# Slots of two experts packed feature-major in one product per tile, and a first up projection that starts on half of the features

## The chip, the cores and the metric

The kernel runs on one core of a Trainium2 chip. The time is that of the device, in microseconds (us), and the profile is one execution of the program. TensorE multiplies matrices, VectorE and ScalarE do elementwise work and evict TensorE's results from its accumulator banks, GpSimd (POOL) and SyncE mostly issue transfers, and 16 DMA engines carry these out. Everything is float32. The profile names TensorE's products PE and its weight loads PEld; the stationary operand of a product is what is loaded, the moving operand streams past it.

## The reference

The reference is one inference step of a two-layer encoder on 288 tokens (256 of a prompt, 32 of a sample) of width 1024. Each layer has an attention part and then a mixture of experts: 16 experts in 4 groups, of which each token uses two.

```
for e in range(N_EXPERTS):
    h = jax.nn.silu(t @ w_gate[e]) * (t @ w_up[e])
    y = y + gate[:, e:e + 1] * (h @ w_down[e])
```

The expert weights (6 MB per expert, 96 MB per layer) are by far the largest input. `gate` is zero except for the two chosen experts of a token, so an expert's product need only be made for the tokens routed to it.

## The kernel before

Tokens lie in three tiles (`TOKS`): 128, 128 and 32 rows of `x_tok`, a token per partition, 1024 features along it. After the attention part, TensorE computes router logits (`route`), and VectorE picks the two experts of each token. For each expert up to 64 tokens are gathered into slots (`CAP = 64`).

The slots of an expert must be there with features on partitions (`xg`, 128 features of 8 blocks by 64 slots), since the features are what the up projection sums over. For experts 2 to 15 the tokens are sorted through DRAM: POOL waits for `sort_row` (L1799), scatters the rows with six indirect DMAs (L2035), loads them back sorted (L2038, L2039, 2.36 MB), TensorE turns them (`turn_rows`, L951), and ScalarE cuts each expert's slots out.

For experts 0 and 1 that would come too late. Their slots are made by products with a 0/1 matrix `pick` (token by 128 slots, 64 of each expert), which VectorE writes last thing before the path in question (L1788). `pack_first` (L935) makes it in two steps. First, for each half of the features, three products (one per token tile) with `pick` stationary and 512 features moving give the slots with tokens on partitions (L939). ScalarE and VectorE copy a half each to `x_first` (L1415, L1801). TensorE runs one filler product of 512 columns (L942, shown at its helper's line L686), transposes the 8 blocks of `x_first` (L948), and ScalarE and VectorE copy the results into `xg` (L1417, L1803). Only then expert 0's up projection starts (`up`, L963, and `expert_up`, L912): 8 feature blocks by 2 halves of the array's columns, products of 512 columns, L916.

The order of the experts' work is written out (`expert_order`): up 0, up 1, down 0, turn the sorted rows, down 1, up 2, then up e and down e - 1 in turn.

Expert weights go into three buffers each for gate and up (4 MB per expert) and for down (2 MB). SyncE issues the loads in the same order (L553 to L559): those of experts 0 to 2 early, that of expert e + 3 when expert e's up projection (`up_done`) or down projection is through. So the load of expert 3's gate and up waits for the end of expert 0's up projection.

## Time and profile before

| | |
|---|---|
| runs, us | 913.27, 915.42, 921.26 (median 915.42) |
| profiled execution, span | 916.5 us, 9955 instructions (the page gives no time of its own around it) |
| TensorE busy | 793.1 us (87%) |
| VectorE, ScalarE, POOL busy | 335.0, 187.3, 44.0 us |
| DMA | 272.80 MB, mean 298 GB/s |
| chain that ended last | PE 56%, DMA 25%, DVE 9%, SyncE's queue 6% |
| mean granted TensorE clock | 0.953 |

Busy time is counted per engine, whether or not something waited for it. The chain that ended last is followed back from the last instruction to what released each step; it says on whom the time depended. The granted clock is the share of TensorE's 2.4 GHz that it was given; its two levels are 1.00 and 0.50 (1.2 GHz).

### The profile page before, as it was taken

Reading aid. Unit: us, or ns where it says so; the run is one execution under the profiler, and the core shown is the slowest. Engines: PE = TensorE matmul, PEld = TensorE weight load, DVE = VectorE, ACT = ScalarE, POOL = GpSimd, SP = SyncE. Lnnn points to the kernel's source line nnn. Section 1 sums busy time; section 2 is a strip of 40 time slices with the busy share of each in tenths; the row PEclk is TensorE's granted clock in tenths of the full one; section 3 lists DMA queues with packets and bytes.
Section 4 is the critical chain, followed back from the end, with each engine's and each line's share of the span. In section 5 each row is a group of like instructions: output and inputs, shape, how many; then the busy total and the mean of one; then the engine's idle time right before and its main releaser. Section 6 shows DMA issues by size and latency. Waiting matters only on the chain.

```text
span 916.5 us, 9955 instructions
## 1 busy us (share of the span) xinstructions
PE 793.1 (87%) x3943; PEld 387.2 (42%) x3943; DVE 335.0 (37%) x749; ACT 187.3 (20%) x452; POOL 44.0 (5%) x58
## 2 busy tenths in 40 slices
PE   6978999998899886876879989979898999777875
PEld 4665777453433222222334567654534333222221
DVE  1016455445422212122281054654533442122138
ACT  1213343110321101110110025620103211111101
POOL 1012000003000000000100000000020000000020
PEclk9998899899999999998989999999989999999998
DMA  9724007736999999999799060581679999999991
GB/s 357 232 72 196 1 1 297 300 153 239 402 424 423 425 428 422 425 426 424 265 350 361 3 261 1 215 330 53 275 282 424 431 423 429 422 428 423 428 398 57
DMA packets 43552, 272.80 MB, mean 298 GB/s; under 512 B 6360, under 2 KB 11166, under 8 KB 25840
## 3 DMA queue, kind: packets, MB, share of 16 engines
q1 hardware_dynamic: 32032, 243.69, 64.6%
q0 software_dynamic: 5888, 19.95, 6.5%
q10 hardware_dynamic: 5584, 8.51, 2.6%
q8 instruction: 32, 0.52, 0.2%
q14 instruction: 16, 0.13, 0.0%
HBM read 253.92 MB, written 18.21 MB: 297 GB/s over the span
## 4 chain that ended last, share of the span: by engine, by line
PE 56%; DMA 25%; DVE 9%; SPq 6%; ACT 2%; issue 1%; ACTq 0%; DVEq 0%
DMA arena<-in_expert_w_up 24%; PE bank L916 16%; PE bank L858 6%; PE bank L930 5%; PE bank L1176 5%; PE bank L845 3%; SPq L502 2%; PE bank L832 2%; PE bank L777 2%; PE bank L939 2%; PE bank L1049 2%; PE bank L825 1%; PE bank L679 1%; PE bank L1141 1%; PE bank L868 1%
## 5 line engine op out<-in xcount | busy, mean ns | idle before, releaser
L916 PE MATMUL bank<-arena 128*64 128x512 f32 x1024 | 240.7, 627 | 48.2 <-DMA arena<-in_expert_w_up 46.5
L916 PEld LDWEIGHTS bank<-arena 128*64 128x64 f32 x1024 | 77.2, 144 | 208.4 <-issue 148.8
L930 PE MATMUL bank<-arena 128*64 128x512 f32 x512 | 116.9, 598 | 16.7 <-DVE arena L1825 16.7
L1825 DVE COPY arena<-bank 128x256 f32<-128x256 f32 x32 | 13.6, 424 | 271.8 <-PE bank L923 271.8
L930 PEld LDWEIGHTS bank<-arena 128*64 128x64 f32 x512 | 34.1, 136 | 77.4 <-issue 54.6
L1378 ACT ACTIVATE arena<-bank 128x256 f32<-128x256 f32 x32 | 12.3, 384 | 265.8 <-PE bank L916 265.8
L1833 DVE RECIPROCAL arena<-arena 128x256 f32<-128x256 f32 x32 | 56.1, 1753 | 1.1
L858 PE MATMUL bank<-arena 128*128 128x512 f32 x128 | 56.0, 595 | 0.0
L1176 PE MATMUL bank<-arena 128*128 128x512 f32 x96 | 43.9, 619 | 6.6 <-ACT arena L1483 5.7
L1234 ACT COPY arena<-bank 128x512 f32<-128x512 f32 (+2 forms) x30 | 15.8, 537 | 112.9 <-PE bank L679 74.2
L858 PEld LDWEIGHTS bank<-arena 128*128 128x128 f32 x128 | 24.0, 190 | 29.6 <-issue 29.5
L1400 ACT COPY arena<-bank 128x512 f32<-128x512 f32 x30 | 17.6, 587 | 91.6 <-PE bank L930 91.6
L845 PE MATMUL bank<-arena 128*128 128x288 f32 x128 | 33.2, 412 | 0.0
L1382 ACT COPY arena<-arena 128x512 f32 x28 | 31.4, 1128 | 8.0 <-issue 7.2
L1176 PEld LDWEIGHTS bank<-arena 128*128 128x128 f32 x96 | 18.9, 199 | 30.3 <-issue 23.4
L1523 DVE COPY arena<-bank 128x512 f32<-128x512 f32 (+3 forms) x20 | 12.9, 649 | 49.5 <-PE bank L679 17.9
L679 PE MATMUL bank<-arena 128*128 128x128 f32 (+1 forms) x144 | 23.1, 320 | 8.0 <-DVE arena L1988 3.2
L1049 PE MATMUL bank<-arena 128*128 128x512 f32 x64 | 28.0, 595 | 1.0 <-DVE arena L1523 1.0
L2024 POOL DMA_DIRECT2D arena<-in_ln_g x4 | 2.3, 567 | 534.6 <-ACT arena L1382 313.5
L845 PEld LDWEIGHTS bank<-arena 128*128 128x128 f32 x128 | 23.7, 190 | 8.5 <-issue 2.7
L679 PEld LDWEIGHTS bank<-arena 128*128 128x128 f32 (+1 forms) x144 | 20.9, 202 | 13.8 <-issue 4.3
L777 PE MATMUL bank<-arena 128*128 128x64 f32 (+1 forms) x172 | 24.0, 280 | 1.3 <-DVE arena L1682 0.5
(272 smaller groups left out, 870.1 us busy)
## 6 DMA issues: line engine op xcount, KB each, us to landing
arena<-in_expert_w_gate SPq DMA_DIRECT2D x32, 2048.0 KB, 20.6
arena<-in_expert_w_up SPq DMA_DIRECT2D x32, 2048.0 KB, 25.6
arena<-in_expert_w_down SPq DMA_DIRECT2D x64, 1024.0 KB, 27.9
arena<-in_w_out SPq DMA_DIRECT2D x4, 2048.0 KB, 9.5
expert_rows<-arena ACTq DMA_DIRECT2D x60, 128.0 KB, 7.9
arena<-in_w_kv_shared SPq DMA_DIRECT2D x3, 2048.0 KB, 10.5
arena<-in_w_mem_kv SPq DMA_DIRECT2D x2, 2048.0 KB, 21.1
arena<-sorted_rows POOLq DMA_DIRECT2D x2, 2048.0 KB, 9.2
```

The lines of the kernel that those rows point to most:

```text
L502: sp.dma_start(g_kv, ins["kv_norm_g"][0].partition_broadcast(P)).then_inc(small_in, 16)
L679: last = tr(b[:, k * n:(k + 1) * n], src[0:n, t, k0 + k::KC], ident[0:n, 0:n])
L777: last = mm(b[:, qt * w:(qt + 1) * w], pt[:, P * i:P * i + P], v[:, kt, h * w:(h + 1) * w], start=(i, kt) == mine_[0], stop=(i, kt) == min ...
L832: last = mm(b[:, 0:NT], w_q[:, k, 4 * g + hh, :], cq_feat[:, k, :], start=k == 0, stop=k == 2)
L845: last = mm(b[:, 0:NT], w_inb[k // 4][:, k % 4, P * c:P * c + P], x_feat[:, k, :], start=k == 0, stop=k == KC - 1)
L858: last = mm(b[:, :], x_feat[:, k, P * t:P * t + P], w_out[k // 4][:, k % 4, 512 * c:512 * (c + 1)], start=k == 0, stop=k == KC - 1)
L916: last = mm(bank[j][64 * half:64 * half + 64, :].rearrange("p (u f) -> p u f", u=2), slots[:, k, 0:CAP], w[:, :, k, 256 * half:256 * half ...
L930: last = mm(bank[3 + j][64 * n:64 * n + 64, :], hid_t[:, j, c, 64 * half:64 * half + 64], w[:, half, c, 512 * n:512 * n + 512], start=(hal ...
L1049: last = mm(b[:, :], feat[:, k, P * t:P * t + P], w[:, k, :], start=k == 0, stop=k == KC - 1)
L1176: last = mm(b[:, :], x_feat[:, k, P * t:P * (t + 1)], w_kvs[c][:, k, :], start=k == 0, stop=k == KC - 1)
L1382: return nc.scalar.copy(xg[:, j], xs[:, bass.ds(at, CAP), :].rearrange("p s k -> p k s"))
L1833: step(V.reciprocal(a, a))
```

## The change

`pack_first` makes the slots feature-major at once: for each of the 8 feature blocks and each token tile, 128 features of `x_tok` (every eighth one) are stationary and the 128 columns of `pick` move. The three products of a block add up in a quarter of an accumulator bank; four blocks fill bank 7, four bank 5. The step over `x_first`, its two copies, the filler product and the transposes go. The first up projection takes its first four feature blocks after ScalarE's copy and waits for VectorE's only before the other four. The second (`up(1)`) has no wait of its own, since it comes behind the first on the same engine.

```
-            def expert_up(j, w, slots):
+            def expert_up(j, w, slots, ks=range(KC)):
-                for k in range(KC):
+                for k in ks:
...
             def pack_first(l):
                 for half in range(2):
-                    for t, (a, n) in enumerate(TOKS):
-                        last = mm(bank[5 + half][:, :], pick[0:n, t, :], x_tok[0:n, t, 512 * half:512 * half + 512],
-                                  start=t == 0, stop=t == 2)
-                    last.then_inc(packed, 1)
-                keep_warm(bank[1], 512)
-                for n, who in enumerate("av"):
-                    pe.wait_ge(first_taken[who], 2 * l + 1)
-                for half in range(2):
                     b = bank[(7, 5)[half]]
                     for k in range(4):
-                        last = tr(b[:, P * k:P * k + P], x_first[:, 4 * half + k::KC], ident)
-                    last.then_inc(first_turned, 1)
+                        for t, (a, n) in enumerate(TOKS):
+                            last = mm(b[:, P * k:P * k + P], x_tok[0:n, t, 4 * half + k::KC], pick[0:n, t, :],
+                                      start=t == 0, stop=t == 2)
+                    last.then_inc(first_packed, 1)
...
-                    if e < 2:
-                        for who in "av":
-                            pe.wait_ge(first_taken[who], 2 * (l + 1))
-                    else:
+                    if e == 0:
+                        for half, who in enumerate("av"):
+                            pe.wait_ge(first_taken[who], l + 1)
+                            last = expert_up(0, ups[0], xg[:, 0], range(4 * half, 4 * half + 4))
+                        last.then_inc(up_done, 1)
+                        return
+                    if e > 1:
                         pe.wait_ge(xg_ready, (NE - 2) * l + e - 1)
...
-                ac.wait_ge(packed, 2 * l + 1)
-                nc.scalar.copy(x_first[:, 0:512], bank[5][:, :]).then_inc(first_taken["a"], 1)
-                ac.wait_ge(first_turned, 2 * l + 1)
+                ac.wait_ge(first_packed, 2 * l + 1)
                 nc.scalar.copy(*first_dst(0)).then_inc(first_taken["a"], 1)
...
-                ve.wait_ge(packed, 2 * l + 2)
-                V.tensor_copy(x_first[:, 512:D], bank[6][:, :]).then_inc(first_taken["v"], 1)
-                ve.wait_ge(first_turned, 2 * l + 2)
+                ve.wait_ge(first_packed, 2 * l + 2)
                 V.tensor_copy(*first_dst(1)).then_inc(first_taken["v"], 1)
```

## Rows read from the trace of the kernel before

**Rows 1.** The page, its first line.
```profile
span 916.5 us, 9955 instructions
```

**Rows 2.** The chain of waits in time: start us, length us, what.
```profile
302.49 32.94 DMA arena<-in_expert_w_up
...
836.78 41.35 DMA arena<-in_expert_w_up
```

**Rows 3.** Windows: stretch, length, busy us per engine, granted clock, DMA share, GB/s.
```profile
227.50:231.50 4.00, 4.00 (x21) 1.56 (x18) 0.61 (x4) 0.09 (x1) 0.07 (x1) 1.00 0.84 291
235.00:236.50 1.50, 1.50 (x10) 0.69 (x8) 0.00 (x0) 0.00 (x0) 0.00 (x0) 1.00 0.76 210
236.50:300.00 63.50, 59.65 (x291) 23.04 (x289) 20.75 (x30) 16.25 (x21) 0.52 (x1) 1.00 1.01 426
300.00:431.00 131.00, 100.75 (x430) 32.24 (x428) 30.78 (x48) 17.78 (x26) 1.09 (x2) 0.95 1.01 425
...
674.50:681.00 6.50, 6.34 (x30) 2.65 (x32) 3.31 (x19) 0.00 (x0) 0.00 (x0) 1.00 0.98 341
681.00:684.50 3.50, 3.50 (x18) 1.38 (x16) 2.23 (x3) 0.38 (x1) 0.00 (x0) 1.00 0.75 174
```

**Rows 4.** Timeline of layer 0's path: start us, length us, engine, line, what.
```profile
214.40 7.00 PE L939 MATMUL bank<-arena 128*128 128x512 f32 x12 [0.45 <-DVE arena L1788]
...
223.45 0.69 DVE L1803 COPY arena<-bank 128x512 f32<-128x512 f32 x1 [1.31 <-PE bank L948]
224.06 0.94 DVE L1805 TENSOR_SCALAR starts<-arena 1x16 int32<-1x16 f32 x5
224.29 13.95 PE L916 MATMUL bank<-arena 128*64 128x512 f32 x64 [0.88 <-DVE arena L1803]
...
231.41 0.33 SPq L528 DMA_DIRECT2D arena<-in_expert_w_gate  x1
```

**Rows 5.** Timeline of layer 1's path.
```profile
661.41 10.37 PE L939 MATMUL bank<-arena 128*128 128x512 f32 x12 [0.58 <-DVE arena L1788]
...
674.66 13.95 PE L916 MATMUL bank<-arena 128*64 128x512 f32 x64 [0.88 <-DVE arena L1803]
...
681.78 0.33 SPq L528 DMA_DIRECT2D arena<-in_expert_w_gate  x1
```

**Rows 6.** Timeline of TensorE's weight loads, both packs, then the routing counts.
```profile
218.91 0.19 PEld L939 LDWEIGHTS bank<-arena 128*128 128x128 f32 x1 [0.24 <-issue]
219.34 0.19 PEld L939 LDWEIGHTS bank<-arena 128*128 128x128 f32 x1 [0.24 <-issue]
220.28 0.29 PEld L939 LDWEIGHTS bank<-arena 32*128 32x128 f32 x2 [0.76 <-issue]
221.34 0.30 PEld L686 LDWEIGHTS bank<-arena 128*128 128x128 f32 x2 [0.76 <-issue]
...
662.43 0.33 PEld L939 LDWEIGHTS bank<-arena 128*128 128x128 f32 x1 [0.52 <-issue]
663.28 0.33 PEld L939 LDWEIGHTS bank<-arena 128*128 128x128 f32 x1 [0.52 <-issue]
665.12 0.50 PEld L939 LDWEIGHTS bank<-arena 32*128 32x128 f32 x2 [1.50 <-issue]
667.12 0.50 PEld L939 LDWEIGHTS bank<-arena 128*128 128x128 f32 x2 [1.50 <-issue]
...
211.57 0.84 PEld L908 LDWEIGHTS bank<-arena 128*128 128x128 f32 x6
```

**Rows 7.** Windows of stretches at half clock, columns as in rows 3.
```profile
213.10:216.40 3.30, 2.85 (x5) 0.96 (x4) 2.53 (x13) 0.00 (x0) 0.00 (x0) 0.50 0.06 25
660.20:670.40 10.20, 9.62 (x11) 2.84 (x10) 2.45 (x13) 0.59 (x1) 5.26 (x6) 0.50 0.48 191
663.60:667.00 3.40, 3.40 (x4) 0.51 (x3) 0.00 (x0) 0.00 (x0) 2.77 (x3) 0.50 0.49 194
158.50:165.20 6.70, 6.15 (x48) 4.50 (x50) 1.51 (x4) 2.83 (x4) 0.00 (x0) 0.50 1.00 411
431.50:434.90 3.40, 3.40 (x10) 0.95 (x8) 0.00 (x0) 0.00 (x0) 0.00 (x0) 0.50 1.02 425
```

More of the change, by code:

```diff
@@ L264, in encoder_step @@
         y_out = zr.cut(2, 512)
-        x_first = Region(y_at).cut(D)
         pair_t = zr.cut(NT)
@@ L309, in encoder_step @@
         tail_ready = sem("tail_ready")
-        packed = sem("packed"); first_turned = sem("first_turned")
+        first_packed = sem("first_packed")
         first_taken = {"a": sem("first_taken_act"), "v": sem("first_taken_dve")}
```

## The prediction

> **What bounds the kernel now.** I read the chain of waits first. In each mixture-of-experts stage it is TensorE until about 302 us (layer 0) and 752 us (layer 1), and from there it is made of waits for expert weights, such as the two in [rows 2]. The windows say why: from 236.5 to 300 us the DMA engines move 426 GB/s and from 300 to 431 us 425 GB/s, without a hole [rows 3]. The loads cannot be shortened, only started earlier. The first load of the saturated stream (expert 3's gate and up weights) is issued by SyncE when expert 0's up projection ends, at 231.41 us and at 681.78 us [rows 4, 5]. So the change is worth what it does to the end of that projection, less what the DMA engines would have been doing anyway.
>
> They were doing something: POOL's load of the sorted rows (576 rows of 4 KB, 2.36 MB). In layer 1 it starts at 674.5 us; 341 GB/s over 6.5 us is 2.22 MB, so it ends near 681.35. The weights come 0.4 us after that, and the 3.5 us from 681 run at 174 GB/s instead of 426 [rows 3]: 3.5 x (1 - 174/426) = 2.07 us lost. In layer 0 it has 1.16 MB by 231.5 (291 GB/s over 4 us) and alone would end near 234.4, three microseconds after the weights are issued; there only 1.5 x (1 - 210/426) = 0.76 us is lost [rows 3]. Call these two losses the slack: no gain can be larger than their sum, 2.8 us.
>
> **The path that changes.** Before: packing starts at 214.40 (layer 0) and 661.41 (layer 1), and expert 0's first product at 224.29 and 674.66: 9.89 and 13.25 us [rows 4, 5]. Packing itself is 7.0 and 10.4 us; the remaining 2.95 us are the filler product, eight transposes and two evictions, the last of which is the 0.69 us of [rows 4]. All of these 2.95 us go.
>
> What comes: 24 products of 128 columns instead of 6 of 512, each again two weight loads and two passes. The columns streamed are the same; the loads are four times as many, 48 instead of 12, and, above all, the order over the token tiles is 128, 128, 32 rows for each of eight feature blocks, where before it was run through twice. [Rows 6] price that. At full clock a pass of 512 columns takes 219.34 - 218.91 = 0.43 us, thus 0.107 us for 128 columns. The two passes on the tile of 32 rows take 221.34 - 220.28 = 1.06 us from load to load, where 0.86 would be the columns: leaving a row size costs 0.20 us. At half clock: 663.28 - 662.43 = 0.85 a pass (0.213 for 128 columns), and 667.12 - 665.12 = 2.00 for two, thus 0.29 per change. That the cost does not shrink with the product is shown by six passes of only 16 columns over the same three tiles (last row of that group): their loads alone take 0.84 us.
>
> A block of features is then 6 passes and 2 changes of row size: 6 x 0.107 + 2 x 0.20 = 1.04 us at full clock, 6 x 0.213 + 2 x 0.29 = 1.86 us at half. Eight blocks: 8.3 us or 14.9 us. The bounds: changes cost nothing (5.1 and 10.2 us), or each change also exposes one more load of 0.107 or 0.213 us (10.0 and 18.3 us). I take the middle, since it is what the rows with both product sizes give.
>
> **Which clock?** The clock decides. It was at half from before the pack in both layers, for 3.4 us in layer 0 and for 10.2 us in layer 1 [rows 7]. In layer 0 it came back after TensorE had run products on all 128 rows up to 216.4. In layer 1 it stayed at half through a stretch in which TensorE had no idle time, but in which half of the passes were on 32 rows (663.6 to 667.0), and came back after the next one, on 128 rows. It also stayed at half through transposes that end on the 32-row tile (158.5 to 165.2) and came back at once after dense expert products (431.5 to 434.9) [rows 7]. The new pack is, without a stop, what it stayed low in: every third product is on 32 rows, and there are two gaps in each block. So I forecast half clock for the whole pack, and for the first 3.4 us of expert 0's up projection, as in 431.5 to 434.9. The other outcome is the first rival.
>
> The Trainium skill ("TensorE: Matmul & The Clock Gate", Part 1) says that the default state is throttled and sustained activity releases it. By that rule, dense work releases it within the pack and the sum is that of rival 1; layer 1's 10.2 us of nearly unbroken work at half clock [rows 7] speak against leaning on it here.
>
> **The sum.** Pack 14.9 us and 0.1 us to the first product: 15.0 against 9.89 and 13.25, thus +5.1 and +1.75 us. The projection itself takes 13.95/2 = 6.97 us at full clock [rows 4]; 3.4 us at half add 1.7. It ends 6.8 and 3.45 us later, and the loads are issued at 238.2 and 685.2 us. Through the DMA: in layer 1 the issue was 0.4 us behind the end of the row load and 2.07 us were lost, so loss = lateness + 1.65. Layer 0: 238.2 - 234.4 + 1.65 = 5.45, less the 0.76 of before: +4.7. Layer 1: 685.2 - 681.35 + 1.65 = 5.5, less 2.07: +3.4. Together +8.1 us, 916.5 -> 924.6 us on the scale of the profiled span [rows 1]. The median of the runs, 915.42, lies 1.1 us below it, so 923.5 us.
>
> Costed at nothing, with their covers. Splitting expert 0's projection: ScalarE's eviction of the first four blocks (0.6 us) hides behind the second half of the pack, VectorE's (0.69 us) behind the projection's first half, at least 3.5 us; uncovered, 0.7 us more. What VectorE does behind that eviction (start columns and flag, some 4 us after 224.06) moves to about 230 to 234.5; its next reader is past expert 0's activation at 238. The sort and the row load hang on VectorE and POOL alone and don't move. Later, TensorE is 4 to 7 us late at turning the rows and at down 0 and 1, but the 8.4 MB of experts 3 and 4 take 20 us, and the next issues come inside them. The late TensorE then waits less at 302 and 752 us.
>
> **Rivals.**
> 1. *The clock comes back inside the pack, as now.* Layer 0: half clock until 216.4, 1.1 blocks, then 6.9 x 1.04: the first product at 223.8, 0.5 us early. Layer 1: half until 670.4, 4.85 blocks, then 3.3 us: 673.8, 0.9 us early. At most 1.4 us gained: 914.0 us. For it: it did so in both layers, and where the filler before the pack falls well it needs little more. Against: the 663.6 to 667.0 stretch. If it happens in one layer only, 4 to 5 us of my sum go: 918 to 919 us. Chance 0.26, most of it for one layer.
> 2. *Changes of row size cost nothing in short products.* Layer 0: 24 products at 0.213 us each and the half-clock part give 220.6; layer 1 gives 671.2; both about 3.5 us early, and denser, so that the clock behaves as now. The gain is capped by the slack: 2.8 us, 912.6 us. Against it stands the last row of [rows 6]. The Trainium skill says both things: its TensorE page (Part 2, Step-by-step) lets the next weights load during the running product, with a time set by columns and not rows, which gives this rival; "TensorEngine Tiling (Array Packing)", Key Properties, says that a change of tiling mode drains the engine, and that is what [rows 6] show. Chance 0.07.
> 3. *Half clock through the whole projection too.* 15.0 + 13.9 us: issues at 243.3 and 690.3 us, 9.8 and 8.5 us lost: 933.7 us. The clock returned sooner in every dense expert stretch of the trace. Chance 0.07.
>
> On the other side of my forecast stands rival 1, in both layers. It decides at the point where the clock is back before the fourth block: 6.9 to 7.0 us of pack is then reachable again.
>
> **How the numbers follow.** Forecast 0.60, 923.5 us; its own range is 919 to 927 us (a pack of 13.5 to 16 us, 2.5 to 6 us of half clock in the projection, in each layer). The range reported is 914 to 927 us: it takes in rival 1 and leaves out rivals 2 and 3 and the tails. A change of over 1%, which is about what a measurement of this kernel can tell from none (its runs spread from 913.27 to 921.26), means below 906.3 or above 924.6 us. Below: no case reaches it, as the slack is 2.8 us; 0.02. Above: rival 3 and somewhat over a quarter of the forecast, 0.23. Within: 0.75.
>
> **What would show it.** In the profile after: 24 products per layer at the new packing line over 14 to 16 us (8 to 9 says rival 1, 5 to 6 says rival 2), weight loads with 0.2 or 0.3 us extra at each tile of 32 rows; a granted clock of 0.50 through the pack and 3 to 4 us on; expert 3's load issued at about 238 and 685 us; a hole in the DMA windows of both layers, about 4 us longer than now in layer 0. The forecast is wrong if the clock is at full speed during the pack, or if the stream of weights starts as early as now.

## The result and the profile after

The changed kernel took 934.89 us (median of 4 runs, 931.67 to 940.89) against 914.35 us (4 runs, 912.94 to 921.26). The medians are 20.5 us apart, a quotient of 1.0225; the ratio on record, which is not that quotient, is 1.0186 with a 95% interval of 1.0129 to 1.0244. Two further measurements of the same kernel, below, gave ratios of 1.0181 and 1.0151, with medians 14.8 and 13.7 us apart. So it is slower by 1.5 to 1.9%, some 14 to 20 us, and outside the predicted range of 914 to 927 us. The direction, and the first product and the load issue both coming later, were as forecast; the size was not.

The profiled execution is the longest of its four runs. These lines of its page are the first one (answering to [rows 1]), the row of engines, the granted clock in 40 slices and the chain by engine:

```profile
span 939.1 us, 10051 instructions
...
PE 822.9 (88%) x3995; PEld 411.5 (44%) x3995; DVE 333.1 (35%) x747; ACT 186.2 (20%) x450; POOL 44.1 (5%) x58
...
PEclk9997899986899989888889999989869999999988
...
PE 58%; DMA 24%; DVE 8%; SPq 6%; ACT 2%; issue 1%; ACTq 0%; DVEq 0%
```

Of the 22.6 us between the two profiled spans, not all is the change. The pack starts at 220.52 us here, 6.1 us later than in [rows 4], behind code that is the same in both kernels: TensorE was at half clock from 203 to 216 us (first row of the windows below). Other executions of the changed kernel start it at 211.8 and 211.3 us, so these 6.1 us belong to this execution and not to the kernel.

The timelines of the two paths, which answer to [rows 4, 5]:

```profile
220.52 16.02 PE L940 MATMUL bank<-arena 128*128 128x128 f32 x48 [0.83 <-DVE arena L1782]
...
236.47 15.66 PE L915 MATMUL bank<-arena 128*64 128x512 f32 x64
...
245.31 0.33 SPq L527 DMA_DIRECT2D arena<-in_expert_w_gate  x1
...
678.41 16.24 PE L940 MATMUL bank<-arena 128*128 128x128 f32 x48 [0.23 <-DVE arena L1782]
...
694.59 15.29 PE L915 MATMUL bank<-arena 128*64 128x512 f32 x64
...
703.06 0.33 SPq L527 DMA_DIRECT2D arena<-in_expert_w_gate  x1
```

From the start of the pack to the first product of the projection it is 15.95 and 16.18 us (9.89 and 13.25 before), and to the issue of expert 3's load 24.8 and 24.65 us (17.0 and 20.4 before). Windows (stretch, length, busy time of TensorE, its loads, VectorE, ScalarE, POOL, then granted clock, DMA share, GB/s) ahead of the first pack, over both packs and over the stretch behind each, which answer to [rows 3, 7]:

```profile
203.00:216.00 13.00, 12.50 (x33) 8.16 (x34) 5.80 (x22) 0.84 (x3) 0.00 (x0) 0.50 0.97 411
216.00:222.90 6.90, 6.07 (x30) 4.41 (x29) 4.08 (x22) 0.00 (x0) 0.12 (x1) 0.99 0.02 8
222.90:239.90 17.00, 17.00 (x49) 11.45 (x50) 2.91 (x14) 0.59 (x1) 6.91 (x8) 0.50 0.71 263
240.00:246.00 6.00, 6.00 (x32) 1.96 (x30) 1.28 (x6) 0.39 (x1) 0.00 (x0) 1.00 0.20 39
676.90:697.30 20.40, 20.16 (x58) 13.47 (x58) 5.01 (x25) 0.59 (x1) 7.03 (x8) 0.50 0.59 217
697.40:704.00 6.60, 6.60 (x34) 2.11 (x32) 2.11 (x10) 0.38 (x1) 0.00 (x0) 1.00 0.17 48
```

In layer 1 the clock is at its half level (0.50) through the whole pack and on into the projection; in layer 0 of this execution the first 2.4 us of the pack, up to 222.9, are at full clock and the rest at half. The pack is hardly shorter for it: 15.96 us to the first product, against 16.17 where all of it is at half. Behind it, the DMA engines carry 39 and 48 GB/s while the sorted rows are in and expert 3's weights are not yet asked for. The weight loads inside the pack, in layer 1 (answering to [rows 6]):

```profile
678.41 1.03 PEld L940 LDWEIGHTS bank<-arena 128*128 128x128 f32 x4 [1.66 <-DVE arena L1782]
...
679.67 0.55 PEld L940 LDWEIGHTS bank<-arena 32*128 32x128 f32 x2 [0.22 <-issue]
680.44 1.03 PEld L940 LDWEIGHTS bank<-arena 128*128 128x128 f32 x4 [0.22 <-issue]
681.70 0.55 PEld L940 LDWEIGHTS bank<-arena 32*128 32x128 f32 x2 [0.22 <-issue]
682.46 1.04 PEld L940 LDWEIGHTS bank<-arena 128*128 128x128 f32 x4 [0.22 <-issue]
```

A block of features takes 680.44 - 678.41 = 2.03 us; the forecast was 1.86.

**Where the time went.** I cut every profiled execution at the same points: start of the pack (P), first product of expert 0 (U), issue of expert 3's load (I), start of expert 15's up projection (the last long wait for weights ends there), start of the next layer's pack, end. All in us:

| kernel | span | layer: U - P | I - P | P to last up | last up of layer 0 to pack of layer 1 | last up of layer 1 to end |
|---|---|---|---|---|---|---|
| before | 916.5 | 9.9 / 13.3 | 17.0 / 20.4 | 216.3 / 216.8 | 230.7 | 38.4 |
| after | 939.1 | 16.0 / 16.2 | 24.8 / 24.6 | 222.0 / 221.8 | 235.9 | 38.9 |

The difference of the spans is 6.1 (ahead of the pack) + 5.7 + 5.2 + 5.0 + 0.5 = 22.5 us. The two layers' 10.7 us were forecast as 8.1. The 5.2 us between the last up projection of layer 0 and the pack of layer 1, where no instruction was changed, were forecast as nothing.

### The profile page after: what moved, and what is told of

Read it like the earlier page. It is cut to its first block, busy times and chain, and to the rows that moved or that the text cites. A ratio compares the mean times of both kernels' runs of the same rounds, so it can differ in the third digit from the quotient of the medians.

```text
span 939.1 us, 10051 instructions
## 1 busy us (share of the span) xinstructions
PE 822.9 (88%) x3995; PEld 411.5 (44%) x3995; DVE 333.1 (35%) x747; ACT 186.2 (20%) x450; POOL 44.1 (5%) x58
## 4 chain that ended last, share of the span: by engine, by line
PE 58%; DMA 24%; DVE 8%; SPq 6%; ACT 2%; issue 1%; ACTq 0%; DVEq 0%
DMA arena<-in_expert_w_up 23%; PE bank L915 16%; PE bank L857 6%; PE bank L929 5%; PE bank L1172 5%; PE bank L940 3%; PE bank L844 3%; SPq L501 2%; PE bank L831 2%; PE bank L776 2%; PE bank L1045 2%; PE bank L678 1%; PE bank L824 1%; PE bank L1137 1%; PE bank L685 1%
## 5 line engine op out<-in xcount | busy, mean ns | idle before, releaser
L915 PE MATMUL bank<-arena 128*64 128x512 f32 x1024 | 246.5, 639 | 44.2 <-DMA arena<-in_expert_w_up 44.2
L929 PE MATMUL bank<-arena 128*64 128x512 f32 x512 | 116.9, 598 | 16.6 <-DVE arena L1817 16.6
L1817 DVE COPY arena<-bank 128x256 f32<-128x256 f32 x32 | 13.6, 424 | 272.1 <-PE bank L922 272.1
L857 PE MATMUL bank<-arena 128*128 128x512 f32 x128 | 56.0, 595 | 0.0
L1172 PE MATMUL bank<-arena 128*128 128x512 f32 x96 | 44.6, 626 | 6.6 <-ACT arena L1477 5.7
L857 PEld LDWEIGHTS bank<-arena 128*128 128x128 f32 x128 | 24.0, 190 | 29.6 <-issue 29.5
L940 PE MATMUL bank<-arena 128*128 128x128 f32 (+1 forms) x96 | 32.3, 492 | 1.1 <-DVE arena L1782 1.1
L1172 PEld LDWEIGHTS bank<-arena 128*128 128x128 f32 x96 | 19.1, 201 | 30.7 <-issue 23.8
L678 PE MATMUL bank<-arena 128*128 128x128 f32 (+1 forms) x144 | 24.4, 332 | 7.9 <-DVE arena L1980 3.2
L1045 PE MATMUL bank<-arena 128*128 128x512 f32 x64 | 30.4, 637 | 1.0 <-DVE arena L1517 1.0
L940 PEld LDWEIGHTS bank<-arena 128*128 128x128 f32 (+1 forms) x96 | 25.2, 326 | 9.8 <-issue 6.2
L678 PEld LDWEIGHTS bank<-arena 128*128 128x128 f32 (+1 forms) x144 | 22.0, 205 | 13.4 <-issue 4.9
## 6 DMA issues: line engine op xcount, KB each, us to landing
arena<-in_expert_w_down SPq DMA_DIRECT2D x64, 1024.0 KB, 26.8
```

The costliest lines, as they stand in the source:

```text
L678: last = tr(b[:, k * n:(k + 1) * n], src[0:n, t, k0 + k::KC], ident[0:n, 0:n])
L857: last = mm(b[:, :], x_feat[:, k, P * t:P * t + P], w_out[k // 4][:, k % 4, 512 * c:512 * (c + 1)], start=k == 0, stop=k == KC - 1)
L915: last = mm(bank[j][64 * half:64 * half + 64, :].rearrange("p (u f) -> p u f", u=2), slots[:, k, 0:CAP], w[:, :, k, 256 * half:256 * half ...
L929: last = mm(bank[3 + j][64 * n:64 * n + 64, :], hid_t[:, j, c, 64 * half:64 * half + 64], w[:, half, c, 512 * n:512 * n + 512], start=(hal ...
L940: last = mm(b[:, P * k:P * k + P], x_tok[0:n, t, 4 * half + k::KC], pick[0:n, t, :], start=t == 0, stop=t == 2)
L1045: last = mm(b[:, :], feat[:, k, P * t:P * t + P], w[:, k, :], start=k == 0, stop=k == KC - 1)
```

## The experiments

Two questions were open. First, what makes the pack long: the half clock (then holding the clock up gives about 8 us, the price in the prediction's first rival), the changes of row size, or something in the short products that the rows of before don't show. Second, what carries a late pack to the end: the late issue of the load alone, or something in the new code (the split projection, the eviction, the longer activity of TensorE) that acts later.

**The changed kernel again.** No edit.

> The changed kernel unaltered, timed again in more rounds. In the two profiles the expert parts answer for 10.7 us of the 22.6 us between the spans (issue of expert 3's load 24.8 and 24.65 us after the start of the pack, against 17.0 and 20.4); the other 12 us lie in stretches whose code is the same, with TensorE more often at half clock. If those 12 us are luck of that one execution, the ratio falls to about 1.012 (10 to 12 us) and the profile shows the earlier stretches as short as before. If the change causes them too, the ratio stays at 1.018 or more.

Measured: 930.67 us against 915.86 us, ratio 1.0181 (1.0164 to 1.0198). Its profiled span is 930.2 us: U - P 16.2 us in both layers, I - P 24.8 and 24.6, P to last up 222.0 and 221.7, between the layers 235.8. The pack starts at 211.84 us. So the 6.1 us ahead of the pack go (the pack even starts 2.6 us earlier than in [rows 4]), and the other columns of the table stay. For the two layers that is the kernel's doing; on the stretch between the layers see the table of all executions below.

**Row sizes in a snake.** Odd blocks run over the tiles backwards, so that one change of row size per block is left instead of two.

```
-                        for t, (a, n) in enumerate(TOKS):
+                        tiles = list(enumerate(TOKS))[::-1 if k % 2 else 1]
+                        for i, (t, (a, n)) in enumerate(tiles):
...
-                                      start=t == 0, stop=t == 2)
+                                      start=i == 0, stop=i == 2)
```

> The three products of a feature block run over the token tiles 128, 128, 32 and in the next block 32, 128, 128: 8 changes of row size per layer instead of 16, the same products. Theory (a change of row size costs 0.29 us at half clock and 0.20 at full, and the clock is held at half by the products on 32 rows): the pack is 8 x 0.29 = 2.3 us shorter, 13.8 us instead of 16.1, still at half clock, and the time some 4 to 5 us shorter than the changed kernel's. Rival (the 48 weight loads of the short products are the price): pack 16 us, time as the changed kernel's.

Measured: U - P 14.10 us in both layers against 16.17, so eight changes of row size cost 2.07 us, 0.26 us each, near the 0.29 of [rows 6]. The clock was at half through the whole pack all the same, with half of the changes of row size gone. The issue came only 1.1 and 0.85 us earlier (I - P 23.7 and 23.8), since 5.0 and 5.2 us of the projection were at half clock instead of 3.1 and 2.7. The time, 929.95 us, ratio 1.0169 (1.0135 to 1.0203), does not resolve so little; the 4 to 5 us that were expected did not come. Between the layers this execution took 239.3 us, the longest of all.

**All tiles on 128 rows.** The third tile is multiplied on 128 rows, with `pick` zero on the 96 rows that are no tokens. No change of row size is left and no product on 32 rows.

```
+                own(V.memset(pick[:, 2, :], 0.0))
...
-                            last = mm(b[:, P * k:P * k + P], x_tok[0:n, t, 4 * half + k::KC], pick[0:n, t, :],
+                            last = mm(b[:, P * k:P * k + P], x_tok[:, t, 4 * half + k::KC], pick[:, t, :],
```

> The third token tile is taken on all 128 rows (the rows past the sample's 32 tokens of the pick matrix are set to zero by one more VectorE instruction), so 24 products of 128 columns all on 128 rows, no change of row size. Theory: 24 x 0.213 = 5.1 us at full clock and 10.2 at half, and the clock comes back inside the pack as it did with the products on 128 rows of the kernel before: pack 6 to 8.5 us, expert 3's load issued 14 to 16 us after the start of the pack, time 911 to 915 us, equal to the kernel before or up to 3 us less. Rival (short products or strided stationary operands themselves are slow, or hold the clock): pack 10 us or more at half clock through to the end, time 922 us or more.

Measured: 919.15 us against 915.86 us, ratio 1.0022 (0.9990 to 1.0053): no loss is resolved any more. The expected pack of 6 to 8.5 us and issue after 14 to 16 us were missed, though, with 11.7 and 18.8. The pack and its windows, and the issue behind it:

```profile
211.28 11.74 PE L940 MATMUL bank<-arena 128*128 128x128 f32 x48 [0.54 <-DVE arena L1783]
...
230.08 0.33 SPq L527 DMA_DIRECT2D arena<-in_expert_w_gate  x1
```

```profile
211.30:216.70 5.40, 5.40 (x22) 5.40 (x23) 1.21 (x7) 0.00 (x0) 2.56 (x3) 0.50 0.26 106
216.90:222.60 5.70, 5.70 (x26) 5.70 (x25) 0.00 (x0) 0.58 (x1) 2.90 (x4) 1.00 0.81 299
```

The reader is to see two things. The clock came back 5.6 us after the start, in both layers, where with products on 32 rows it stayed at half to the end of the pack. The edit takes away two things at once, the products on 32 rows and the changes of row size; the snake, with half of the changes and all of the 32-row products, stayed at half. And the pack hardly cared: from one pass to the next it is 0.240 us in the first window, at half clock, and 0.238 in the second, at full clock, though the DMA engines carry 106 GB/s in the one and 299 in the other. All 48 passes take 11.7 us, 0.243 us each with the start. By the prediction's prices a pass would be 0.213 us at half clock and 0.107 at full. With 0.243 a pass, a block of the changed pack is 6 x 0.243 + 2 x 0.29 = 2.04 us, near the measured 2.03: the changes of row size had the forecast price and the passes had not.

**A longer filler ahead of the pack**, to hold the clock up.

```
-                keep_warm(bank[1], 2048)
+                keep_warm(bank[1], 3072)
```

> The changed kernel with the filler product that runs while VectorE ranks the experts lengthened from 2048 to 3072 columns, so that TensorE has no 2 us of idle time before the pack and its clock does not fall. Theory: at full clock the pack takes 8 x 1.04 = 8.3 us, 0.5 us less than the kernel before from pack to first product in layer 0; time 912 to 917 us. Rival (clock not decisive, the changes of row size alone are): pack stays above 12 us and the time above 924 us. A third: the longer filler runs at half clock and holds up the ranking by up to 2 us per layer.

Measured: 933.76 us, ratio 1.0207 (1.0177 to 1.0237), and neither theory was tested as meant. In layer 0 the clock fell at 212.6 us all the same, 1.3 us before the pack; in layer 1 most of the filler itself ran at half clock (653.0 to 666.5 us), and the clock fell again 0.7 us behind the start of the pack. U - P stayed at 16.2 us in both layers, I - P became 24.8 and 25.8, P to last up 222.0 and 222.9. A filler that costs more when the clock is low is no safe way to keep it high.

**The kernel before, again.** No edit.

> The kernel before, unaltered, for a second profile. Two profiles of the changed kernel and one of the padded kernel show the stretch from the last up projection of layer 0 to the pack of layer 1 as 235.8 us and 230.7 us (before: 230.7). If that stretch goes with the kernel and not with luck, it is 230.7 us again here; if it is luck, it differs by several us. Layer 1's pack-to-issue is 17 us if the long half clock of the first profile (20.4 us) was luck, 20.4 if not.

Measured: 920.82 us (one run; the kernel before had a median of 919.19 in the same comparison). Here both layers had the 10.2 us of half clock that only layer 1 has in [rows 7]: U - P 13.3 us in both, I - P 20.4 in both. P to last up stayed 216.8 and 216.9 us, between the layers 230.3. So an issue 3.4 us later than in layer 0 of [rows 4] costs 0.5 us. The 20.4 us of [rows 5] were not luck of layer 1, then; it is the 17.0 us of layer 0 that an execution may or may not have.

**The price of a short product by itself.** In the kernel before, layer 0, four series of 128-column products into an unused bank, behind dense fillers, so that the clock is at full (each loop is written on one line here): stationary operand spread (every eighth float32 of a row), stationary operand contiguous, moving operand spread, and contiguous with the row size alternating.

```
+    for k in range(KC): mm(out, x_tok[:, 0, k::KC], pick[:, 0, :], start=True, stop=True)            # L696
+    for k in range(KC): mm(out, x_tok[:, 0, P * k:P * k + P], pick[:, 0, :], start=True, stop=True)  # L699
+    for k in range(KC): mm(out, pick[:, 0, :], x_tok[:, 0, k::KC], start=True, stop=True)            # L702
+    for k in range(4):
+        mm(out, x_tok[:, 0, P * k:P * k + P], pick[:, 0, :], start=True, stop=True)                  # L705
+        mm(out, x_tok[0:32, 2, P * k:P * k + P], pick[0:32, 2, :], start=True, stop=True)            # L706
```

> The kernel before with four series of short products in layer 0 after the transposes, each behind five dense filler products and written to the filler's bank: 8 with 128 stationary features taken at every eighth element and the pick matrix moving (the changed kernel's form); 8 with 128 neighbouring features stationary; 8 with the pick matrix stationary and every eighth feature moving; 8 alternating between 128 and 32 rows with neighbouring features. Padded, a pass of the changed kernel's form took 0.24 us at full clock and at half. If the spread stationary operand is the price, the first series is 0.24 us a pass and the second and third 0.11 us. If it is the spread operand on either side, the third is 0.24 us too. If it is two-pass products of 128 columns as such, all are 0.24 us. The fourth shows a change of row size at 0.2 to 0.3 us by itself.

Windows of the first two series, then lines by their instructions (duration in ns as min/median/max, first and last start), then the loads of the alternating series in time:

```profile
222.10:225.70 3.60, 3.60 (x17) 3.50 (x15) 0.51 (x3) 0.00 (x0) 0.29 (x1) 1.00 0.76 240
230.10:231.90 1.80, 1.80 (x17) 1.73 (x16) 0.00 (x0) 0.00 (x0) 0.00 (x0) 1.00 0.08 18
```

```profile
L696 PEld LDWEIGHTS bank<-arena x16: 312/335/336, 221.8 to 225.5; 128*128 128x128 f32 x16
L699 PEld LDWEIGHTS bank<-arena x16: 190/192/192, 229.7 to 231.7; 128*128 128x128 f32 x16
...
L702 PEld LDWEIGHTS bank<-arena x16: 190/208/208, 235.8 to 239.5; 128*128 128x128 f32 x16
L702 PE MATMUL bank<-arena x16: 392/413/413, 236.2 to 239.7; 128*128 128x128 f32 x16
```

```profile
244.58 0.29 PEld L706 LDWEIGHTS bank<-arena 32*128 32x128 f32 x2
244.99 0.30 PEld L705 LDWEIGHTS bank<-arena 128*128 128x128 f32 x2
245.41 0.29 PEld L706 LDWEIGHTS bank<-arena 32*128 32x128 f32 x2
```

At full clock the same product takes 0.238 us a pass with the stationary operand spread, 0.112 with it contiguous, and 0.233 with the moving operand spread ((239.7 - 236.2)/15); the first two are the median steps from one pass to the next. The loads of a spread stationary operand take 335 ns against 192. Two contiguous passes with a change take 0.41 us, so a change costs 0.41 - 0.22 = 0.19 us, as [rows 6] priced it. This settles the pack: the spread read, at 0.24 us a pass, is what full clock did not speed up, and the short contiguous pass is as cheap at full clock as forecast (at half clock no contiguous product of 128 columns was run).

It holds for products, not for every read with that step. The eight transposes of the kernel before, which took `x_first` at the same step of eight elements, cost 1.11 us together:

```profile
222.30 1.11 PE L948 MATMUL bank<-arena 128*128 128x128 f32 x8
```

That is some 0.11 us from one to the next, one pass each, with weight loads of 193 ns. Why a transpose is spared is not shown. The whole kernel with the series, whose layer 0 the series delay, took 943.92 us (one run).

**The kernel before with a padded pack.** The old two-step pack, its third tile on 128 rows; same edit as above, on L939.

```
+                own(V.memset(pick[:, 2, :], 0.0))
...
-                        last = mm(bank[5 + half][:, :], pick[0:n, t, :], x_tok[0:n, t, 512 * half:512 * half + 512],
+                        last = mm(bank[5 + half][:, :], pick[:, t, :], x_tok[:, t, 512 * half:512 * half + 512],
```

> The kernel before with its third token tile on all 128 rows (rows past the 32 tokens of the pick matrix zeroed), so 6 products of 512 columns without a change of row size. Theory (products on 32 rows hold the clock at half): the clock is back at the latest 5.5 us after the start of the pack in both layers, the pack takes 6 to 8 us instead of 7.0 and 10.4, time 0 to 3 us less than before. Rival (the rows make no difference to the clock): half clock for some 9 us of layer 1 again, time as before.

Measured: 918.56 us against 919.19 us, ratio 0.9984 (0.9945 to 1.0022). I - P fell to 15.4 and 18.2 us (17.0 and 20.4 before), P to last up stayed 216.0 and 216.5. An issue that comes 1.6 and 2.2 us earlier moves the end of the layer by 0.3 us: in front of the kernel before there is next to nothing to gain, as the prediction's slack had it. The clock did as expected: in layer 1 it came back 5.6 us after the start of the pack instead of 9.0, with nothing changed but the 96 empty rows and the changes of row size. The profiled execution, 928.8 us, is one of this kernel's two longest; its stretch between the layers took 238.1 us, without any lateness.

**The kernel before, only late.** A filler behind the transposes, of nine (first kernel) and of ten products of 512 columns (second, shown); everything else is the kernel before.

```
                     last.then_inc(first_turned, 1)
+                keep_warm(bank[1], 10 * 512)
```

> The kernel before with nine dense filler products (9 x 0.85 = 7.7 us at full clock) between its transposes and expert 0's up projection, in both layers: the pack and everything else as before, only the start of expert 0's projection is as late as in the changed kernel. Theory (the whole loss of the changed kernel comes from that lateness: late weight loads, and a shift of the later stages against the points at which the clock falls): expert 3's load is issued 24 to 26 us after the start of the pack, the stretch between the layers is about 235 us again, time 927 to 933 us. Rival (something else in the changed kernel costs the other half): 5.6 us later in layer 0 and 4 to 7 in layer 1, the stretch between the layers stays at 230.7 us, time 922 to 926 us.

> The kernel before with ten dense filler products (8.5 us) after its transposes, which makes it issue expert 3's load as late as the changed kernel does (24.6 us after the start of the pack; nine gave 23.8 and 24.4). Theory (lateness of that issue is the whole cause): its ratio to the kernel before is that of the changed kernel, 1.018, within 0.3%. Rival (the changed kernel has a further cost of its own): 1.011 to 1.013, as nine fillers gave on another chip (1.0104), and the changed kernel 4 us or more above it.

Measured with 9: I - P 23.8 and 24.4 us, 927.48 us, ratio 1.0104 (1.0068 to 1.0140). With 10: I - P 24.5 and 23.65 us, 933.28 us, ratio 1.0154 (1.0121 to 1.0187). Beside the latter, on the same chip, the changed kernel:

> The changed kernel once more, on the same chip as the delayed one, so that the two can be set against each other. 1.018 of the kernel before again; last weights of layer 0's experts wanted 222 us after the start of its pack (before: 216.3 and 216.8).

Measured: 932.38 us, ratio 1.0151 (1.0120 to 1.0182); I - P 24.8 and 24.8 us. The same ratio from the old code with nothing but a late end is the answer to the second question: the lateness is enough. That it is all is not shown to better than some 4 us. With nine fillers the issue came 1.0 and 0.4 us before that of the changed kernel, and the ratio, 1.0104, has an interval that ends at 1.0140, below 1.0151, though it overlaps that of the changed kernel. And with ten, the profiled execution (928.56 us) is the second shortest of six, with a median of 933.28. P to last up is 222.1 and 220.5 us with the filler and 222.3 and 221.7 in the changed kernel, and the stretch between the layers is 234.8 in both, 4 us longer than the 230.3 and 230.7 of the two executions of before. The chain of waits in that stretch, near layer 1's routing, first of the late kernel before with ten fillers, then of the second repeat of the changed one:

```profile
654.58 3.23 PE bank L883 x16
657.80 6.39 PE bank L686 x8
```

```profile
655.01 3.23 PE bank L882 x16
658.24 6.42 PE bank L685 x8
```

In the kernel before, the same 16 products took 1.94 us (first fence), and the granted clock of a window over them was 1.00 (second); the window of the late kernel before (third) and that of the changed one (fourth) show 0.54:

```profile
649.88 1.94 PE bank L883 x16
```

```profile
650.00:658.00 8.00, 5.88 (x29) 3.65 (x30) 5.19 (x22) 0.25 (x2) 0.00 (x0) 1.00 0.98 419
```

```profile
649.00:664.00 15.00, 14.26 (x44) 9.40 (x44) 7.69 (x26) 1.80 (x5) 0.00 (x0) 0.54 0.93 392
```

```profile
649.00:664.00 15.00, 14.23 (x47) 9.62 (x47) 7.77 (x24) 2.24 (x5) 0.00 (x0) 0.54 0.94 399
```

Here TensorE is on the chain, and it runs at half clock where it ran at full (before, all of 644 to 659 us is at 1.00 too). The same fall, from 18.1 to 4.5 us before the pack, stands ahead of layer 0's pack in the first profile of the changed kernel (203 to 216 us), and there nothing was late yet; ahead of layer 1's pack the first profile and the first repeat do not have it.

**The changed kernel without the split projection.** Expert 0's projection waits for both evictions and runs through.

```
                     if e == 0:
-                        for half, who in enumerate("av"):
+                        for who in "av":
                             pe.wait_ge(first_taken[who], l + 1)
-                            last = expert_up(0, ups[0], xg[:, 0], range(4 * half, 4 * half + 4))
-                        last.then_inc(up_done, 1)
-                        return
```

> The changed kernel's pack alone: expert 0's up projection waits for both evictions, as before, instead of starting on half of the features. VectorE's eviction (0.69 us and the hand-over) is then uncovered: first product 0.75 us later after the pack, issue about 25.5 us after its start, all of it on the path: 1 to 2 us above the changed kernel. If the split is worth nothing, no difference.

Measured: 932.00 us, ratio 1.0142 (1.0110 to 1.0173), the same as the changed kernel's 1.0151. U - P is 17.1 us in both layers, 1.0 more than with the split, I - P 26.9 and 26.8, P to last up 224.1 and 224.0; between the layers it was 233.5, 1.3 less. The split hides 1 us of eviction, as it says; its worth in the whole time is below what was resolved. The other 1 us by which the issue came later is the clock, at half for 5.4 and 5.2 us of the projection instead of 3.0 and 3.5.

**The best of both.** The old pack, padded, without its own filler, and with the split projection.

```
+                own(V.memset(pick[:, 2, :], 0.0))
...
-                keep_warm(bank[1], 512)
...
+                    if e == 0:
+                        for half, who in enumerate("av"):
+                            pe.wait_ge(first_taken[who], 2 * (l + 1))
+                            last = expert_up(0, ups[0], xg[:, 0], range(4 * half, 4 * half + 4))
```

> The kernel before with the third tile on all 128 rows, without the filler between products and transposes, and with the first up projection split over the halves of the features (the change's second part, on the old pack). Issue 1.5 to 2 us earlier than the padded kernel's 15.4 and 18.2 us after the start of the pack. Theory (the row load keeps the DMA engines busy until 20 us after the start of the pack): the last weights of layer 0 still land 216 us after the start of the pack and the time is that of the kernel before within 0.3%. Rival (an earlier issue is worth its size): 3 to 5 us less than the kernel before.

Measured: 917.50 us against 918.66 us, ratio 0.9994 (0.9968 to 1.0021). U - P was 8.6 us in both layers, 4.6 us less than the long case of before, and I - P 15.75 in both. P to last up: 217.2 and 216.1. Nothing came of it. No version beat the kernel before by more than the measurement can tell.

**All executions on one line.** P to last up against I - P, both layers of each:

| kernel | I - P | P to last up |
|---|---|---|
| old pack padded, split | 15.75 / 15.7 | 217.2 / 216.1 |
| old pack padded | 15.4 / 18.2 | 216.0 / 216.5 |
| before | 17.0 / 20.4 | 216.3 / 216.8 |
| new pack on 128 rows | 18.8 / 18.8 | 216.3 / 216.3 |
| before, again | 20.4 / 20.4 | 216.8 / 216.9 |
| snake | 23.7 / 23.8 | 221.4 / 220.8 |
| before, 9 fillers late | 23.8 / 24.4 | 220.9 / 221.4 |
| before, 10 fillers late | 24.5 / 23.7 | 222.1 / 220.5 |
| changed (three executions) | 24.6 to 24.8 | 221.7 to 222.3 |
| longer filler | 24.8 / 25.8 | 222.0 / 222.9 |
| no split | 26.9 / 26.8 | 224.1 / 224.0 |
| with the four series, layer 0 | 49.8 | 246.9 |

Down to 15.4 us the length does not fall below 216 us, the bound that the prediction drew from the load of the sorted rows. From 23.7 us on it is I - P plus 197.2 us within 0.5 us, up to the last row. The corner lies near 20 us: at 20.4 the length is 216.8, up by 0.5. And the kernel before stood on it in one layer and 3 us ahead of it in the other.

**The stretches that were not changed.** The same executions, with the start of layer 0's pack, the time from the last up projection of layer 0 to the pack of layer 1, and the mean granted clock in it:

| kernel | pack starts at | between the layers | clock there |
|---|---|---|---|
| before | 214.4 | 230.7 | 0.97 |
| before, again | 216.7 | 230.3 | 0.97 |
| new pack on 128 rows | 211.3 | 230.7 | 0.96 |
| with the four series (layer 0 30 us late) | 209.3 | 230.3 | 0.96 |
| old pack padded, split | 209.2 | 233.4 | 0.95 |
| no split | 214.3 | 233.5 | 0.95 |
| changed, second repeat | 211.3 | 234.9 | 0.93 |
| before, 10 fillers late | 211.1 | 234.8 | 0.93 |
| before, 9 fillers late | 209.4 | 235.3 | 0.94 |
| changed, first repeat | 211.8 | 235.8 | 0.93 |
| changed | 220.5 | 235.9 | 0.93 |
| longer filler | 213.9 | 236.8 | 0.93 |
| old pack padded | 218.0 | 238.1 | 0.93 |
| snake | 209.4 | 239.3 | 0.92 |

The length goes with the clock: 0.96 to 0.97 for 230.3 to 230.7 us, 0.92 to 0.95 for everything longer. All eight executions with an issue 23.7 to 26.9 us after the pack have 233.5 us or more, but so have, within 0.1 us, two of the six others.

## Why the prediction was wrong

**The bound and the direction: right.** The load of expert 3's weights is what the time hangs on, a gain is capped by the row load in front of it, and a late end of the first projection is lost one for one. The prediction's conversion (lateness less about 2.1 us in layer 0, one for one in layer 1) applied to the measured lateness of 7.8 and 4.3 us gives 5.7 and 4.2; measured were 5.7 and 5.0.

**The clock: right.** It was at half through the pack in both layers, but for the first 2.4 us in layer 0, and for 3.4 and 2.7 us of the projection; 3.4 was forecast. Its first rival, the clock back inside the pack and 8.3 us of pack at full clock, did not occur, and its price was false as well: the padded pack had full clock for more than half of its length and took 11.7 us. At full clock the changed pack would be 8 x (6 x 0.24 + 2 x 0.20) = 14.7 us, an estimate from the four series. So the sentence that the clock decides holds for the projection behind the pack and not for the pack itself: by this estimate 1.5 us of pack lie between its two levels, not the 6.6 (14.9 - 8.3) of the prediction.

**The failed step of the pack's sum: "0.107 us for 128 columns", and "0.213".** It scaled a pass of 512 contiguous columns down to 128. The new product reads its stationary operand at every eighth float32, and then a pass takes 0.24 us at either clock. From this step came 2.02 us a block instead of 1.86, a first product after 16.0 to 16.2 us instead of 15.0, and the issue at P + 24.6 to 24.8 us instead of P + 23.8: about 1 us in each layer, 2 of the missing microseconds. The price of a change of row size held (0.19 us alone at full clock, 0.26 in the snake at half), so the second rival, by which changes cost nothing, did not occur. The Trainium skill's TensorE page ("TensorE: Matmul & The Clock Gate", LDWEIGHTS) has the load's time depend on its columns alone; 335 against 192 ns for the same 128 columns contradict that. The Trainium skill's "SBUF — State Buffer" (Door 1, the note on cachelines) says that reads keep full bandwidth within a line of 16 bytes, four float32, and pay for each line that they cross into. This operand steps 32 bytes, and the passes of 0.238 and 0.233 us instead of 0.112 agree with it, for the stationary and the moving side; the kernel before's transposes, with the same step at some 0.11 us, do not. The prediction did not weigh that rule, and it was the one that spoke against the change.

**The failed step of the whole: work that comes late later costs nothing.** "Later, TensorE is 4 to 7 us late ... the next issues come inside them" holds within each layer, as the table shows. For the stretch between the layers, where TensorE and VectorE set the end and no weights do, the prediction had no term at all: it put unchanged code at unchanged time. The runs showed 234.9 to 235.9 us there in three executions of the changed kernel against 230.7 and 230.3, thus 4.2 to 5.6 us more, and the late kernels before showed 234.8 and 235.3 without any of the new code. One window over the whole stretch, of before and then of the changed kernel, says what is longer in it:

```profile
430.70:661.40 230.70, 206.11 (x1145) 120.64 (x1145) 102.21 (x240) 55.56 (x183) 6.76 (x8) 0.97 0.58 218
```

```profile
442.50:678.40 235.90, 211.82 (x1145) 123.40 (x1145) 102.20 (x240) 55.55 (x183) 6.76 (x8) 0.93 0.57 213
```

The same 1,145 passes and the same VectorE, ScalarE and POOL time; only TensorE is busy 5.7 us longer, at a mean clock of 0.93 instead of 0.97, and the stretch is 5.2 us longer. In the first repeat of the changed kernel an attention step of layer 1 shows it in the chain (first fence), beside the row of before (second); the mean clock over these two stretches was 0.85 and 1.00:

```profile
458.46 16.34 PE bank L1045 x32
```

```profile
454.23 13.97 PE bank L1049 x32
```

Why the clock falls in other places is not shown. It is not that the stretch starts later: it starts at 433.5 us in the second profile of before and at 433.5 and 433.8 in the two repeats of the changed kernel, with 230.3 against 234.9 and 235.8 us. It is not a matter of more lateness, more loss: with layer 0 delayed by 30 us the stretch took 230.3 us. And it comes without lateness: the two padded old packs took 233.4 and 238.1. So a lower clock as the way in which the stretch gets longer is shown; that lateness brings it on is a tendency, eight of eight executions against two of six, with its inner cause open.

**The sum again.** The second repeat of the changed kernel (span 929.3 us) against the mean of the two executions of before (917.75): layer 0 222.3 - 216.55 = 5.7, between the layers 234.85 - 230.5 = 4.35, layer 1 221.65 - 216.85 = 4.8, the end 39.2 - 38.3 = 0.9 (unexplained; the late kernels before have 38.3), and ahead of the first pack 211.3 - 215.55 = -4.3: 11.5 us between the spans, where the medians of the runs differ by 13.7 (932.38 - 918.66). The forecast had 8.1, all of it in the layers. There 10.5 was measured, 2.4 more, from the price of a pass above all. What the unchanged stretches add is known less well: in this pair the 4.35 us between the layers are balanced by 4.3 us ahead of the pack, where no change can have acted yet, and the medians of the two repeats leave 3.9 (first repeat) and 2.3 us (second) for them beside the layers and the end. No run says how much of that would be there in an average execution.

**The chances.** 0.23 for slower by over 1% came in part from the third rival, the clock staying low through the whole projection. Its 933.7 us are near the measured 934.89, but by luck: it had the issues at 243.3 and 690.3 us, 28.9 us behind the start of the pack, and they came after 24.8 and 24.65. What was missing was any case in which unchanged code gets slower. The bounds of the pack, 10.2 to 18.3 us, held. A small misreading: what follows the pack in the kernel before is 2.9 us (9.89 - 7.00, 13.25 - 10.37) and not 2.95; it does not enter the sum.

## What to carry to other kernels

Price a float32 product by the stride of both its operands, not only by rows and columns, and from a row with that stride and that kind of instruction: packing feature-major saved transposes and two evictions and paid for it in a read at every eighth element. Plot the end of a stage against the issue that starts its stream before optimizing what lies in front: here it was flat for some 4 us and then rose one for one, so that nothing was to be gained and much to be lost. And leave room in the range for the clock of stages that a change doesn't touch: one unchanged stretch of 230 us took up to 9 us more in some executions.

## What the hardware showed

- A float32 pass of 128 columns takes 0.112 us with contiguous operands, 0.238 with the stationary and 0.233 with the moving one at a stride of eight elements, at full clock; at half clock the pass with the spread stationary operand takes 0.240, so the clock hardly touches it. Transposes over the same stride take some 0.11 at full clock.
- In a pack without idle time, in which every third product was on 32 rows, the clock stayed at half to the end (for 13.6 to 16.2 us); when the same products ran on 128 rows it was back after 5.6 us, in both layers. In the old pack the same padding brought it back after 5.6 us instead of 9.0 (layer 1). Whether the rows or the changes of row size count is not separated. The padding is one VectorE memset.
- A change between products on 128 and on 32 rows costs 0.19 us at full clock and 0.26 to 0.29 at half, each way.
